# Moving the block exchange of an MLP's hidden layer from GpSimd's queue to SyncE's, with other buffers and take times

## The chip, the core and the metric

The kernel runs on one core of a Trainium2 chip. Its time is the device time of one execution in microseconds (us). Before the change it is 2130.66 us, the median of three runs (2129.62 to 2133.73). The engines are PE (TensorE), DVE (VectorE), ACT (ScalarE), POOL (GpSimd) and SP (SyncE). SP computes nothing here; it issues DMAs.

## The reference

Two transformer blocks follow each other on 256 tokens of width 2048, everything in fp32. Both end in an MLP with a squared ReLU and a hidden width of 8192; the change touches only these two MLPs.

```python
def sqrelu_mlp(h, w1, w2):                       # block 1
    return jnp.square(jax.nn.relu(h @ w1)) @ w2

x = x + g1 * rms_norm(fourier_mix(modulate(rms_norm(x, g), sh1, sc1)) @ fnet_w_out, g)
x = x + g2 * rms_norm(sqrelu_mlp(modulate(rms_norm(x, g), sh2, sc2), w_mlp_in, w_mlp_out), g)
# sh, sc, g1 and g2 are silu(c) @ w_mod + b_mod

x = x + mixed @ w_out                            # block 2: attention
u = jax.nn.relu(rmsnorm(x, g_mlp) @ w_up)
x = x + (u * u) @ w_down
return rmsnorm(x, g_final)
```

## The kernel before

**Weights.** Every weight is read once from HBM by SP in chunks of 1 MB: 512 rows by 512 columns, in a ring of four slots, `raw` (L334 to L343). Before it loads a slot again, SP waits until DVE has finished with the chunk four places earlier (`raw_used`). A chunk is used in two halves. For each half ACT rounds it to fp32r (`w_high`, `high_part`, L900), DVE subtracts for the rest (`w_low`, `low_part`, L1267), and PE multiplies three times (high by high, low by high, high by low; L495 to L497), which gives 12 matmuls of 512 columns. `w_high` and `w_low` have four slots (LEAD = 4), so ACT can prepare half n + 4 only once PE is done with half n.

**An MLP** is cut into four quarters of 2048 hidden columns. A quarter has 64 halves: 32 for the up projection, in four steps c = 0 to 3 of 512 columns (8 halves each), and 32 for the down projection. The order of the halves is a table (`QUARTER_ORDER`). The very first quarter has another (`FIRST_ORDER`): halves 0 to 11 are the first four of each of the steps 0, 1 and 2, halves 12 to 23 the last four of each, 24 to 31 step 3. So its steps end at halves 15, 19, 23 and 31, and those of the other quarters at 7, 15, 23 and 31. Loads of another weight (`w_mod`, for the vector g2) lie among the loads of the first two quarters: SP issues such a tile behind chunk pos + 2 for each pos in `MOD_FIRST` or `MOD_AFTER`, and DVE sums it up in one operation of 2048 columns (L1279).

**Turning the hidden layer.** The down projection needs the hidden values turned, so that hidden columns lie on the partitions. After the last half of a step, ACT applies ReLU (L982, L1019) and squares in place (`hidden`, L984, L1021), DVE transposes 32x32 blocks (`turn_blocks`, L1433) from `hidden` into `blocks`, and 16 DMAs of 32 KB (`exchange`, L436) bring the blocks from each group of 32 partitions to the others (`extra<-scr` in the profile: `exchanged` lies in `extra`, `hidden` and `blocks` in `scr`). Each moves one run of 256 numbers (1 KB) per partition. POOL issues them and does nothing else in that time. Then ACT copies the result into `u_high` (`take_exchanged`, L959) and DVE puts the rest into `u_low` (`take_low`, L1425). The tables `FIRST_TAKES` and `TAKES` say behind which half's weights ACT and DVE do this: 5, 6, 7 and 6 halves behind the end of steps 0 to 3 in the first quarter, and 6 halves behind it in all others. `FIRST_BLOCKS` puts the transposes 0, 1, 2 and 0 halves behind the end.

ACT and DVE execute what is written in their order. An ACT that waits for an exchange prepares no weights, and after four halves PE has none.

Of the kernel before, what the change touches and what calls it, by code (L numbers as in the profile page):

```python
# [29 lines left out]
TT = SEQ // P  # L30
KT = D // P
CW = 512
# [66 lines left out]
FIRST_TAKES = {y + d: c for c, (y, d) in enumerate(zip(FIRST_UP_ENDS, (5, 6, 7, 6)))}  # L99
FIRST_BLOCKS = {y + d: c for c, (y, d) in enumerate(zip(FIRST_UP_ENDS, (0, 1, 2, 0)))}  # L100
TAKES = {y + 6: c for c, y in enumerate(UP_ENDS)}
DOWN_ENDS = [QUARTER_ORDER.index((NC + c, HALVES - 1)) for c in range(NC)]
AFTER = {DOWN_ENDS[1] + 2: 0, DOWN_ENDS[1] + 4: 1, DOWN_ENDS[2] + 2: 2}
EARLY_UP = sum(unit == UP for unit, _ in FRONT)
# [5 lines left out]
RUN = TT * CW // QUADS  # L110
# [62 lines left out]
def program(nc, x, c_in, w_mod, b_mod, norm_g, w_mlp_in, w_mlp_out, fnet_w, g_attn, w_in, b_f,  # L173
# [8 lines left out]
    with ctx:  # L182
# [78 lines left out]
        hidden = scr[:, 0:TT * CW].rearrange("p (t n) -> p t n", t=TT)  # L261
        tables = extra[:, :].rearrange("p (t n) -> p t n", t=2)
        turned = extra[:, 0:2 * CW].rearrange("p (b n) -> p b n", b=2)
        blocks = scr[:, TT * CW:2 * TT * CW]
# [64 lines left out]
        def _(eng):  # L329
# [36 lines left out]

            for n, (unit, k) in enumerate(FRONT):
# [9 lines left out]
            for pos in range(EARLY_UP - 2, 32):  # L377
# [4 lines left out]
                if pos in MOD_FIRST:  # L382
                    mod_tile(G2, MOD_FIRST.index(pos))
            for pos in range(32):
# [4 lines left out]
                if pos in MOD_AFTER:  # L389
                    mod_tile(G2, len(MOD_FIRST) + MOD_AFTER.index(pos))  # L390
            for q in range(2, QUARTERS):
                for ch in range(2, 32):
                    mlp_chunk(w_mlp_in, w_mlp_out, q, ch)
                for j in range(2):
# [14 lines left out]
            with t.loop(eng, 0, QUARTERS - 1, raw=32) as q:  # L409
                for ch in range(2, 32):  # L410
                    mlp_chunk(w_up, w_down, q, ch)
                for j in range(2):
                    chunk(w_up, j * 4 * P, (q + 1) * D)
            for ch in range(2, 32):
                mlp_chunk(w_up, w_down, QUARTERS - 1, ch)

# [10 lines left out]
        def _(eng):  # L427
            t = Tally()

            def exchange(c):  # L430

                t.add("blocks")
                eng.wait_ge(t_blocks, t.c["blocks"])
                for a in range(QUADS):
                    for q in range(QUADS):
                        eng.dma_start(exchanged[q * BLOCK:(q + 1) * BLOCK, a * RUN:(a + 1) * RUN],  # L436
                                      blocks[a * BLOCK:(a + 1) * BLOCK, q * RUN:(q + 1) * RUN])\
                           .then_inc(t_exchanged[c % 2], 16)

# [21 lines left out]
            for q in range(QUARTERS):  # L461
                for c in range(NC):
                    exchange(c)
# [1339 lines left out]
```

## Time and profile before

| | us |
|---|---|
| median of three runs | 2130.66 |
| the profiled execution | 2133.73 |
| its span (first to last instruction) | 2131.9 |
| PE busy | 2040.6 |
| DVE busy | 1285.1 |
| ACT busy | 1029.4 |
| POOL busy (only issues and clears) | 273.1 |

The profiled execution is the slowest of the three runs. Its span and the 1.8 us around it make its time. PE's share of the span is 96%. Its mean granted clock is 0.984 of full speed. The stretch from about 311 to 402 us belongs to the first quarter of the first MLP, that up to 985 us to the rest of that MLP, 1000 to 1400 us to attention, and 1430 to 2115 us to the second MLP.

### The profile page before, as it was taken

To read this page: it belongs to the slowest core of one execution; us is meant where nothing else is said; L and a number is where in the kernel's file an instruction comes from. 1 tells how busy PE (TensorE), PEld (TensorE's weight loads), DVE (VectorE), ACT (ScalarE), POOL (GpSimd) and SP (SyncE) were. 2 spreads that over 40 slices of the span, in tenths; PEclk is the share of its full clock that TensorE was granted. 3 is DMA by queue.
4 is the path that set the end of the run, shared out by engine and by line. 5 is a ranking of instruction groups with operands and counts; after the bars stand their busy time and mean duration, and the time that the engine had idled before them with its cause. 6 is when DMAs were issued, how large, how long until landed. Compare 5 with 4: busy or idle time off the path is not lost.

```text
span 2131.9 us, 23074 instructions
## 1 busy us (share of the span) xinstructions
PE 2040.6 (96%) x8965; PEld 1652.8 (78%) x8965; DVE 1285.1 (60%) x1259; ACT 1029.4 (48%) x1350; POOL 273.1 (13%) x537
## 2 busy tenths in 40 slices
PE   3999879999999999998999999999999999999997
PEld 1776567788888888887788777788888888888886
DVE  7989776657665554556446555655555554554554
ACT  3333434445444544545555745555445544544553
POOL 0000014102202301210000000002202301310410
PEclk9899889999999999999999999999999999999999
DMA  9999897778766656664545444457656656666762
GB/s 401 408 384 365 318 342 254 269 244 271 268 233 194 221 198 203 212 198 137 178 158 170 146 158 158 159 177 217 217 190 203 219 197 203 214 200 193 225 207 99
DMA packets 214262, 480.23 MB, mean 225 GB/s; under 512 B 15592, under 2 KB 16040, under 8 KB 205328
## 3 DMA queue, kind: packets, MB, share of 16 engines
q1 hardware_dynamic: 195904, 455.11, 63.2%
q0 software_dynamic: 17232, 20.51, 3.3%
q10 hardware_dynamic: 1024, 3.20, 0.4%
q8 instruction: 71, 1.16, 0.2%
q14 instruction: 31, 0.25, 0.0%
HBM read 459.87 MB, written 2.10 MB: 217 GB/s over the span
## 4 chain that ended last, share of the span: by engine, by line
PE 80%; DVE 7%; DMA 7%; ACT 3%; issue 2%; POOL 1%; ACTq 0%; SPq 0%; DVEq 0%
PE ps L495 25%; PE ps L497 25%; PE ps L496 25%; DVE w_low L1267 2%; DVE scr L1279 2%; DMA raw<-in_fnet_w 2%; DMA raw<-in_w_mod 2%; DMA raw<-in_w_mlp_in 1%; POOL extra L436 1%; DVE scr L1294 1%; ACT w_high L900 1%; DMA extra<-scr 1%; PE ps L513 1%; PE ps L550 1%; PE ps L526 1%
## 5 line engine op out<-in xcount | busy, mean ns | idle before, releaser
L1267 DVE TENSOR_TENSOR w_low<-raw,w_high 128x1024 fp32r<-128x1024 f32 x672 | 817.0, 1222 | 676.1 <-ACT w_high L900 675.7
L900 ACT ACTIVATE w_high<-raw 128x1024 fp32r<-128x1024 f32 x672 | 706.2, 1058 | 881.0 <-PE ps L497 773.7
L495 PE MATMUL ps<-w_high,h_both 128*128 128x512 f32 x1536 | 608.9, 396 | 16.2 <-DVE w_low L1267 10.5
L497 PE MATMUL ps<-w_high,h_both 128*128 128x512 f32 x1536 | 600.9, 391 | 0.0
L496 PE MATMUL ps<-w_low,h_both 128*128 128x512 f32 x1536 | 600.7, 391 | 0.0
L495 PE MATMUL ps<-w_high,u_high 128*128 128x512 f32 x1152 | 449.7, 390 | 3.9 <-DVE w_low L1267 3.6
L497 PE MATMUL ps<-w_high,u_low 128*128 128x512 f32 x1152 | 448.3, 389 | 0.0
L496 PE MATMUL ps<-w_low,u_high 128*128 128x512 f32 x1152 | 448.3, 389 | 0.0
L436 POOL DMA_DIRECT2D extra<-scr x512 | 250.1, 497 | 1044.5 <-DVE scr L1433 800.2
L495 PEld LDWEIGHTS ps<-w_high,h_both 128*128 128x128 f32 x1536 | 290.4, 189 | 79.5 <-DVE w_low L1267 10.5
L497 PEld LDWEIGHTS ps<-w_high,h_both 128*128 128x128 f32 x1536 | 290.0, 189 | 61.5
L496 PEld LDWEIGHTS ps<-w_low,h_both 128*128 128x128 f32 x1536 | 290.6, 189 | 60.2 <-issue 1.4
L495 PEld LDWEIGHTS ps<-w_high,u_high 128*128 128x128 f32 x1152 | 216.3, 188 | 50.2 <-DVE w_low L1267 3.8
L497 PEld LDWEIGHTS ps<-w_high,u_low 128*128 128x128 f32 x1152 | 216.2, 188 | 45.0
L496 PEld LDWEIGHTS ps<-w_low,u_high 128*128 128x128 f32 x1152 | 216.3, 188 | 44.7
L1279 DVE SCALAR_TENSOR_TENSOR scr<-raw,silu_c,scr 128x2048 f32<-128x2048 f32 x64 | 150.4, 2351 | 10.6 <-DMA raw<-in_w_mod 5.5
L1294 DVE SCALAR_TENSOR_TENSOR scr<-raw,silu_c,scr 128x1024 f32<-128x1024 f32 x46 | 59.1, 1284 | 9.3 <-DMA raw<-in_w_mod 7.1
L1425 DVE TENSOR_TENSOR u_low<-extra,u_high 128x512 fp32r<-128x512 f32 x64 | 41.2, 686 | 30.3 <-ACT u_high L959 30.3
L1433 DVE STREAM_TRANSPOSE scr<-scr 128x512 f32<-128x512 f32 x64 | 41.8, 691 | 25.6 <-ACT scr L1021 24.0
L959 ACT ACTIVATE u_high<-extra 128x512 fp32r<-128x512 f32 x64 | 36.6, 619 | 39.6 <-DMA extra<-scr 39.6
L608 PE MATMUL ps<-extra,acc 128*128 128x512 f32 x64 | 31.3, 649 | 23.1 <-ACT acc L1050 23.1
L910 ACT ACTIVATE junk<-xs 128x512 f32<-128x512 f32 x64 | 40.4, 632 | 24.0 <-DVE xs L1405 16.0
(183 smaller groups left out, 846.2 us busy)
## 6 DMA issues: line engine op xcount, KB each, us to landing
raw<-in_w_mod SPq DMA_DIRECT2D x96, 1024.0 KB, 7.2
raw<-in_w_mlp_in SPq DMA_DIRECT2D x64, 1024.0 KB, 5.9
raw<-in_w_mlp_out SPq DMA_DIRECT2D x64, 1024.0 KB, 5.3
raw<-in_w_up SPq DMA_DIRECT2D x64, 1024.0 KB, 5.4
raw<-in_w_down SPq DMA_DIRECT2D x64, 1024.0 KB, 5.1
raw<-in_w_in SPq DMA_DIRECT2D x48, 1024.0 KB, 5.1
raw<-in_fnet_w SPq DMA_DIRECT2D x16, 1024.0 KB, 7.0
extra<-scr POOLq DMA_DIRECT2D x512, 32.0 KB, 3.9
```

What stands on the lines that cost most here:

```text
L436: eng.dma_start(exchanged[q * BLOCK:(q + 1) * BLOCK, a * RUN:(a + 1) * RUN], blocks[a * BLOCK:(a + 1) * BLOCK, q * RUN:(q + 1) * RUN])\
L495: eng.matmul(dst, ah, wh, start=(k == 0), stop=False)
L496: eng.matmul(dst, ah, wl, start=False, stop=False)
L497: last = eng.matmul(dst, al, wh, start=False, stop=(k == KT - 1))
L900: eng.activation(w_high[:, h % LEAD, :], raw[:, slot, (h % 2) * 2 * CW:(h % 2 + 1) * 2 * CW], ACT.Copy).then_inc(high_ready, 1)
L910: eng.activation(junk[:, :], src, ACT.Square, accum_out=ssq[:, column:column + 1])\
L959: eng.activation(dst, src[:, tt, :, :, :], ACT.Copy).then_inc(t_high, 1)
L1267: eng.tensor_tensor(w_low[:, h % LEAD, :], raw[:, slot, piece], w_high[:, h % LEAD, :].bitcast(f32), ALU.subtract).then_inc(raw_used if h ...
L1279: eng.scalar_tensor_tensor(out=mod_acc(v), in0=raw[:, slot, :], scalar=silu_c[:, bass.ds(kk, 1)], in1=mod_acc(v), op0=ALU.mult, op1=ALU.ad ...
L1294: ins = eng.scalar_tensor_tensor(out=sums, in0=raw[:, slot, k * HALF:(k + 1) * HALF], scalar=silu_c[:, 2 * r + k:2 * r + k + 1], in1=other ...
L1425: eng.tensor_tensor(low, src[:, tt, :, :, :], high.bitcast(f32), ALU.subtract).then_inc(t_low, 1)
L1433: last = eng.transpose(dst[:, tt, :, :, :], hidden[:, tt, :].rearrange("p (k q i) -> p k q i", k=4, q=QUADS))
```

## The change

- The 16 DMAs of an exchange are issued by SP. They stand in SP's order behind the load of chunk y // 2 + 6 of the quarter, where y is the half at which the step ends (`EXCHANGED_BEHIND = 6`), and behind a `w_mod` tile where one follows this chunk. The first waits for `t_blocks`, the semaphore of the block transposes.
- Each of them now moves four runs of 64 numbers (256 bytes) per partition on both sides, where it was one run of 256 numbers. `blocks` and `exchanged` are laid out accordingly: DVE's transposes write `128x16x32` in one pattern.
- `relu` and `hidden` are two buffers now; `blocks` shares its place with `relu`. ACT no longer waits for `t_blocks` ahead of the ReLU.
- The takes stand 4 halves behind the end of a step in the first quarter (before: 5, 6, 7, 6) and 5 in all others (before: 6). `FIRST_BLOCKS` is gone: the transposes stand at the end of the step itself.

```diff
-FIRST_TAKES = {y + d: c for c, (y, d) in enumerate(zip(FIRST_UP_ENDS, (5, 6, 7, 6)))}
-FIRST_BLOCKS = {y + d: c for c, (y, d) in enumerate(zip(FIRST_UP_ENDS, (0, 1, 2, 0)))}
-TAKES = {y + 6: c for c, y in enumerate(UP_ENDS)}
+FIRST_TAKES = {y + 4: c for c, y in enumerate(FIRST_UP_ENDS)}
+TAKES = {y + 5: c for c, y in enumerate(UP_ENDS)}
+EXCHANGED_BEHIND = 6
...
-        hidden = scr[:, 0:TT * CW].rearrange("p (t n) -> p t n", t=TT)
+        relu = scr[:, 0:TT * CW].rearrange("p (t n) -> p t n", t=TT)
+        hidden = scr[:, TT * CW:2 * TT * CW].rearrange("p (t n) -> p t n", t=TT)
-        blocks = scr[:, TT * CW:2 * TT * CW]
+        blocks = scr[:, 0:TT * CW]
...
+            def exchange(c):                       # on SP
+                t.add("blocks")
+                eng.wait_ge(t_blocks, t.at("blocks", 0))
+                for a in range(QUADS):
+                    src = blocks[a * BLOCK:(a + 1) * BLOCK, :].rearrange("p (k q n) -> p k q n", k=4, q=QUADS)
+                    for q in range(QUADS):
+                        dst = exchanged[q * BLOCK:(q + 1) * BLOCK, :].rearrange("p (k a n) -> p k a n", k=4, a=QUADS)
+                        eng.dma_start(dst[:, :, a, :], src[:, :, q, :]).then_inc(t_exchanged[c % 2], 16)
+            def exchange_behind(ch):
+                for c, y in enumerate(UP_ENDS):
+                    if ch == y // 2 + EXCHANGED_BEHIND:
+                        exchange(c)
...
                 if pos in MOD_FIRST:
                     mod_tile(G2, MOD_FIRST.index(pos))
+                for c, y in enumerate(FIRST_UP_ENDS):
+                    if pos + 2 == y // 2 + EXCHANGED_BEHIND:
+                        exchange(c)
...
                 if pos in MOD_AFTER:
                     mod_tile(G2, len(MOD_FIRST) + MOD_AFTER.index(pos))
+                exchange_behind(pos + 2)
...
-            def exchange(c):                       # on POOL
-                t.add("blocks")
-                eng.wait_ge(t_blocks, t.c["blocks"])
-                for a in range(QUADS):
-                    for q in range(QUADS):
-                        eng.dma_start(exchanged[q * BLOCK:(q + 1) * BLOCK, a * RUN:(a + 1) * RUN],
-                                      blocks[a * BLOCK:(a + 1) * BLOCK, q * RUN:(q + 1) * RUN])\
-                           .then_inc(t_exchanged[c % 2], 16)
...
-                            if t.c["up"] > 1:
-                                eng.wait_ge(t_blocks, t.c["up"] - 1)
-                            eng.activation(hidden, ps[:, bank:bank + 2, :], ACT.Relu).then_inc(up_taken, 1)
+                            eng.activation(relu, ps[:, bank:bank + 2, :], ACT.Relu).then_inc(up_taken, 1)
                             eng.wait_ge(up_taken, t.c["up"])
-                            eng.activation(hidden, hidden, ACT.Square).then_inc(up_ready, 1)
+                            eng.activation(hidden, relu, ACT.Square).then_inc(up_ready, 1)
...
-                dst = blocks.rearrange("p (q k t j) -> p t k q j", q=QUADS, k=4, t=TT)
+                dst = blocks.rearrange("p (b t j) -> p t b j", t=TT, j=BLOCK)
...
-                    if y in FIRST_BLOCKS:
+                    if hh == 7 and c < NC:
                         turn_blocks()
```

SP in the first quarter, from the `w_mod` tile behind chunk 10 on. `raw` is the ring of weight slots, `in_w_mlp_in` and `in_w_mlp_out` are the up and the down projection's weights. In the kernel before no exchange stands here:

```order
L342 DMA raw<-in_w_mod 128x2048 [waits raw_used]
L342 DMA raw<-in_w_mlp_in 128x4x512 [waits raw_used] x3
L342 DMA raw<-in_w_mod 128x2048 [waits raw_used]
L342 DMA raw<-in_w_mlp_in 128x4x512 [waits raw_used] x2
L342 DMA raw<-in_w_mlp_out 128x4x512 [waits raw_used]
L342 DMA raw<-in_w_mod 128x2048 [waits raw_used]
L342 DMA raw<-in_w_mlp_out 128x4x512 [waits raw_used] x3
```

The three loads in a row are chunks 11, 12 and 13; then come the tile behind chunk 13, chunks 14 and 15, chunk 16 with its tile, and chunks 17 to 19. In the changed kernel the same place reads:

```order
L342 DMA raw<-in_w_mod 128x2048 [waits raw_used]
L342 DMA raw<-in_w_mlp_in 128x4x512 [waits raw_used] x3
L342 DMA raw<-in_w_mod 128x2048 [waits raw_used]
L375 DMA extra<-scr 32x4x64 [waits t_blocks]
L375 DMA extra<-scr 32x4x64 x15
L342 DMA raw<-in_w_mlp_in 128x4x512 [waits raw_used] x2
L375 DMA extra<-scr 32x4x64 [waits t_blocks]
L375 DMA extra<-scr 32x4x64 x15
L342 DMA raw<-in_w_mlp_out 128x4x512 [waits raw_used]
L342 DMA raw<-in_w_mod 128x2048 [waits raw_used]
L342 DMA raw<-in_w_mlp_out 128x4x512 [waits raw_used]
L375 DMA extra<-scr 32x4x64 [waits t_blocks]
```

The exchanges of steps 0, 1 and 2 now stand behind a load that itself waits for DVE: the `w_mod` tile behind chunk 13, chunk 15 and chunk 17.

ACT in the first quarter, in the kernel before, from the ReLU of step 0 (`scr<-ps`) to the take of step 1 (`u_high<-extra`):

```order
L982 ACTIVATE scr<-ps 128x1024
L984 ACTIVATE scr<-scr 128x1024
L900 ACTIVATE w_high<-raw 128x1024 x4
L982 ACTIVATE scr<-ps 128x1024
L984 ACTIVATE scr<-scr 128x1024
L900 ACTIVATE w_high<-raw 128x1024
L959 ACTIVATE u_high<-extra 128x4x128 x2
L900 ACTIVATE w_high<-raw 128x1024 x3
L982 ACTIVATE scr<-ps 128x1024
L984 ACTIVATE scr<-scr 128x1024
L900 ACTIVATE w_high<-raw 128x1024 x2
L959 ACTIVATE u_high<-extra 128x4x128 x2
```

And in the changed kernel, from the same ReLU to the same take and the weights behind it:

```order
L984 ACTIVATE scr<-ps 128x1024
L986 ACTIVATE scr<-scr 128x1024
L904 ACTIVATE w_high<-raw 128x1024 x4
L963 ACTIVATE u_high<-extra 128x4x128 x2
L984 ACTIVATE scr<-ps 128x1024
L986 ACTIVATE scr<-scr 128x1024
L904 ACTIVATE w_high<-raw 128x1024 x4
L963 ACTIVATE u_high<-extra 128x4x128 x2
L984 ACTIVATE scr<-ps 128x1024
L986 ACTIVATE scr<-scr 128x1024
L904 ACTIVATE w_high<-raw 128x1024 x4
```

The take of step 0 was one weight half behind the ReLU and square of step 1 and is now ahead of them; the take of step 1 was two halves behind those of step 2 and is now ahead of them.

## Rows read from the trace of the kernel before

**Rows 1.** The page's part 1: busy time, share, instructions.
```profile
PE 2040.6 (96%) x8965; PEld 1652.8 (78%) x8965; DVE 1285.1 (60%) x1259; ACT 1029.4 (48%) x1350; POOL 273.1 (13%) x537
```

**Rows 2.** Busy time in stretches, then PE's granted clock, DMA share, GB/s.
```profile
402.00:985.00 583.00, 583.00 (x2566) 481.50 (x2566) 341.35 (x297) 282.45 (x322) 93.79 (x192) 1.00 0.70 226
1430.00:2115.00 685.00, 685.00 (x3024) 567.22 (x3023) 367.32 (x334) 336.82 (x391) 125.07 (x256) 1.00 0.63 200
```

**Rows 3.** PE from 343 to 385 us: start, time, idle before it.
```profile
365.05 0.50 PE L495 MATMUL ps<-w_high,h_both 128*128 128x512 f32 x1 [2.41 <-DVE w_low L1267]
382.35 0.50 PE L495 MATMUL ps<-w_high,u_high 128*128 128x512 f32 x1 [3.41 <-DVE w_low L1267]
```

**Rows 4.** All waits: us in total, times, longest.
```profile
ACT u_high L959 <- DMA extra<-scr: 39.6, 12, 9.7
```

**Rows 5.** ACT from 318 to 402 us, in order of time.
```profile
324.59 1.06 ACT L900 ACTIVATE w_high<-raw 128x1024 fp32r<-128x1024 f32 x1 [1.60 <-PE ps L497]
...
335.47 1.06 ACT L900 ACTIVATE w_high<-raw 128x1024 fp32r<-128x1024 f32 x1 [1.59 <-PE ps L497]
336.44 1.01 ACT L982 ACTIVATE scr<-ps 128x1024 f32<-128x1024 f32 x1
337.48 1.06 ACT L984 ACTIVATE scr<-scr 128x1024 f32<-128x1024 f32 x1
338.45 1.04 ACT L900 ACTIVATE w_high<-raw 128x1024 fp32r<-128x1024 f32 x1
342.64 1.15 ACT L959 ACTIVATE u_high<-extra 128x512 fp32r<-128x512 f32 x2 [3.15 <-DMA extra<-scr]
...
346.35 1.06 ACT L900 ACTIVATE w_high<-raw 128x1024 fp32r<-128x1024 f32 x1 [0.67 <-PE ps L497]
...
360.72 1.16 ACT L959 ACTIVATE u_high<-extra 128x512 fp32r<-128x512 f32 x2 [7.86 <-DMA extra<-scr]
...
378.95 1.15 ACT L959 ACTIVATE u_high<-extra 128x512 fp32r<-128x512 f32 x2 [9.72 <-DMA extra<-scr]
```

**Rows 6.** DVE from 318 to 402 us.
```profile
327.70 1.31 DVE L1433 STREAM_TRANSPOSE scr<-scr 128x512 f32<-128x512 f32 x2 [0.78 <-ACT scr L984]
...
332.49 2.35 DVE L1279 SCALAR_TENSOR_TENSOR scr<-raw,silu_c,scr 128x2048 f32<-128x2048 f32 x1
...
336.57 1.23 DVE L1267 TENSOR_TENSOR w_low<-raw,w_high 128x1024 fp32r<-128x1024 f32 x1 [0.59 <-ACT w_high L900]
...
343.30 1.30 DVE L1425 TENSOR_TENSOR u_low<-extra,u_high 128x512 fp32r<-128x512 f32 x2 [2.56 <-ACT u_high L959]
```

**Rows 7.** SP from 318 to 402 us; one row can hold several issues.
```profile
334.87 0.34 SPq L342 DMA_DIRECT2D raw<-in_w_mod  x1
337.82 9.49 SPq L342 DMA_DIRECT2D raw<-in_w_mlp_in  x2
```

**Rows 8.** Line 342: duration of an issue in ns, min/median/max.
```profile
L342 SPq DMA_DIRECT2D raw<-in_w_mod x96: 327/340/470, 0.8 to 595.4; - x96
L342 SPq DMA_DIRECT2D raw<-in_w_mlp_in x64: 367/368/467, 227.6 to 870.4; - x64
```

**Rows 9.** Line 436: the same, and the time from issue to landing.
```profile
L436 POOL DMA_DIRECT2D extra<-scr x512: 496/496/522, 329.3 to 2048.5; - x171
...
DMA to landing us min/median/max: 1.7/3.9/7.4
```

**Rows 10.** The chain of waits, 322 to 385 us: start, us, what.
```profile
336.64 5.97 DMA extra<-scr
...
353.42 7.28 DMA extra<-scr
```

**Rows 11.** DMA queues: packets, MB, share of 16 engines' span.
```profile
q0 software_dynamic: 17232, 20.51, 3.3%
```

**Rows 12.** PE from 990 to 1000 us, in order of time.
```profile
992.94 3.67 PE L550 MATMUL ps<-cst,xs 128*128 128x128 f32 x16 [5.21 <-DVE xs L1373]
```

**Rows 13.** Busy time in the ten us behind it; columns as in Rows 2.
```profile
992.00:1002.00 10.00, 8.10 (x27) 6.81 (x28) 9.44 (x17) 4.37 (x16) 0.00 (x0) 0.51 0.33 105
```

More of the change, by code:

```diff
@@ L109 @@
 QUADS = P // BLOCK
-RUN = TT * CW // QUADS
 MOVED = 16 * QUADS * QUADS * NC // 2
@@ L393, in _ @@
                     mlp_chunk(w_mlp_in, w_mlp_out, q, ch)
+                    exchange_behind(ch)
                 for j in range(2):
@@ L408, in _ @@
             chunk(w_up, 4 * P, 0)
-            with t.loop(eng, 0, QUARTERS - 1, raw=32) as q:
+            with t.loop(eng, 0, QUARTERS - 1, raw=32, blocks=NC) as q:
                 for ch in range(2, 32):
                     mlp_chunk(w_up, w_down, q, ch)
+                    exchange_behind(ch)
                 for j in range(2):
@@ L415, in _ @@
                 mlp_chunk(w_up, w_down, QUARTERS - 1, ch)
+                exchange_behind(ch)
             outv = out.rearrange("(t p) n -> p t n", p=P)
@@ L427, in _ @@
         def _(eng):
-            t = Tally()
-            def exchange(c):
-                t.add("blocks")
-                eng.wait_ge(t_blocks, t.c["blocks"])
-                for a in range(QUADS):
-                    for q in range(QUADS):
-                        eng.dma_start(exchanged[q * BLOCK:(q + 1) * BLOCK, a * RUN:(a + 1) * RUN],
-                                      blocks[a * BLOCK:(a + 1) * BLOCK, q * RUN:(q + 1) * RUN])\
-                           .then_inc(t_exchanged[c % 2], 16)
             for v, unit in enumerate(MOD_INIT):
@@ L460, in _ @@
             eng.memset(acc[:, :, :], 0.0).then_inc(acc_zero, 1)
-            for q in range(QUARTERS):
-                for c in range(NC):
-                    exchange(c)
             eng.wait_ge(mod_read, G2 + 1)
@@ L468, in _ @@
             eng.dma_start(grow[:, :], g_final.broadcast_to([P, D])).then_inc(grow_in, 16)
-            for q in range(QUARTERS):
-                for c in range(NC):
-                    exchange(c)
         @block.tensor
@@ L955, in take_exchanged @@
                 eng.wait_ge(t_exchanged[c % 2], 16 * QUADS * QUADS * (c // 2 + 1) + earlier)
-                src = exchanged.rearrange("p (a k t j) -> p t k a j", k=4, a=QUADS, t=TT)
+                src = exchanged.rearrange("p (k a t j) -> p t k a j", k=4, a=QUADS, t=TT)
                 for tt in range(TT):
@@ L1011, in mlp_body @@
                             t.add("up")
-                            eng.wait_ge(t_blocks, t.at("up", -1))
                             if scaled:
                                 for tt in range(TT):
-                                    last = eng.activation(hidden[:, tt, :], lin(c)[:, tt, :], ACT.Relu,
+                                    last = eng.activation(relu[:, tt, :], lin(c)[:, tt, :], ACT.Relu,
                                                           scale=rstd[:, tt:tt + 1])
@@ L1018, in mlp_body @@
                             else:
-                                eng.activation(hidden, lin(c), ACT.Relu).then_inc(up_taken, 1)
+                                eng.activation(relu, lin(c), ACT.Relu).then_inc(up_taken, 1)
                             eng.wait_ge(up_taken, t.at("up", 0))
-                            eng.activation(hidden, hidden, ACT.Square).then_inc(up_ready, 1)
+                            eng.activation(hidden, relu, ACT.Square).then_inc(up_ready, 1)
                         else:
@@ L1416, in take_low @@
             def take_low(c):
-                src = exchanged.rearrange("p (a k t j) -> p t k a j", k=4, a=QUADS, t=TT)
+                src = exchanged.rearrange("p (k a t j) -> p t k a j", k=4, a=QUADS, t=TT)
                 for tt in range(TT):
@@ L1430, in turn_blocks @@
                 eng.wait_ge(up_ready, t.at("up", 0))
-                dst = blocks.rearrange("p (q k t j) -> p t k q j", q=QUADS, k=4, t=TT)
+                dst = blocks.rearrange("p (b t j) -> p t b j", t=TT, j=BLOCK)
                 for tt in range(TT):
-                    last = eng.transpose(dst[:, tt, :, :, :],
-                                         hidden[:, tt, :].rearrange("p (k q i) -> p k q i", k=4, q=QUADS))
+                    last = eng.transpose(dst[:, tt, :, :], hidden[:, tt, :].rearrange("p (b i) -> p b i", i=BLOCK))
                 last.then_inc(t_blocks, 1)
```

## The prediction, made before the changed kernel was run

> **What bounds the kernel now.** I read the page's first part, then stretches of time, then what PE waited for. PE is busy for 96% of the span [rows 1], and in the two long stretches that hold 7 of the 8 MLP quarters it is never idle: 583.00 of 583.00 us and 685.00 of 685.00 us [rows 2]. POOL's exchanges, DVE's transposes and ACT's copies all lie in these stretches too, and cost nothing. The first of them gives the kernel's beat: 583.00 us over 2566 matmuls is 0.227 us each, so a half (12 matmuls) takes 2.73 us and a chunk 5.45 us. What the change can win must therefore lie in the first quarter, from 311 to 402 us. There PE waits twice for DVE's `w_low`, 2.41 and 3.41 us, and once more for 0.2 [rows 3]: 6.0 us together. DVE waits for ACT, and ACT for the exchange: 39.6 us over the whole kernel, of which 3.15, 7.86 and 9.72 us stand at the takes of steps 0, 1 and 2 [rows 4, 5]. POOL is slow at this, 16 issues of 0.496 us or 7.9 us [rows 9], and behind its last issue the data still took 5.97 and 7.28 us to land [rows 10]. The gain can be no more than 6.0 us, 0.28% of the time. The loss has no such bound.
>
> **The change, part by part.**
>
> *Quarters without these stalls (7 of 8).* Behind the end of a step ACT needs about 2.1 us for ReLU and square [rows 5] and DVE 1.3 for the transposes [rows 6], so the blocks are ready some 4.5 us behind the end. SP by then has loaded the chunk ahead and issues 16 DMAs. One issue costs SP 0.34 us for a tile in 128 long rows and 0.37 for a chunk in 512 short ones [rows 8]; the new DMAs have 128 pieces, so I take 0.37, or 5.9 us for 16. With some 2 us until the last has landed (POOL's shortest are 1.7 [rows 9], when nothing is queued) an exchange takes L = 7.9 us and ends 12.4 us behind the step. ACT comes to its take when the copy behind half 5 is made, 5 x 2.73 + 1.0 = 14.6 us behind it. Nobody waits. SP's next load can be late by about 3 us, but a load is needed three chunks (16 us) later: hidden. In the second quarter the `w_mod` tiles push the exchange back; the worst is step 1, where it stands behind a tile that waits until DVE is done with the tile three chunks earlier, 10.1 us behind the step. There it ends at 18.3, ACT waits 3.7 us, and PE's four prepared halves last until 24.5: hidden, as long as L stays under about 10.6. So these edits cost 0. The dropped wait for `t_blocks`, the second buffer, the other pattern of the transposes (the same 512 numbers per operation) also get 0: ACT and DVE are 48% and 60% busy, PE's work hides them. POOL's 250 us of issues go, but no engine waited for POOL other than by the exchange.
>
> *The first quarter.* Its steps end only 4 halves (10.9 us) apart, and here the exchange now starts late and the take stands early. I follow it with these durations: copy high 1.0, ReLU 1.0, square 1.05, take 1.15 on ACT; `take_low` and the transposes 1.3 each, `w_low` 1.2, a `w_mod` tile 2.35 on DVE [rows 5, 6].
>
> Step 0. Half 15 ends at 324.5 and half 19 at 335.4, when ACT starts the next copies [rows 5]. SP reaches the exchange behind the tile of chunk 13, which it can issue only when DVE is done with the tile before (332.49 + 2.35); it did so at 334.87 [rows 6, 7]. The exchange runs 335.2 to 341.1 and has landed by 343.0. POOL's landed at 342.6, so nothing is won. But ACT now meets this take ahead of the ReLU of step 1 and ahead of the copy for half 24, which before stood at 338.45. It waits from 336.4 to 343.0, does take, ReLU and square until 346.2 and the copy until 347.1; DVE's transposes end at 347.5 and `w_low` of half 24 at 348.7. PE was done with half 23 at 346.3 [rows 5]: it waits 2.4 us.
>
> Step 1. Its exchange stands behind chunk 15, which needs DVE's second half of chunk 12, done at 349.9. It runs from 350.6 to 356.5 and lands at 358.5. Then take, ReLU of step 2, square, copy (362.6), and on DVE `w_low` at 364.2. PE, started again at 348.7, runs out at 359.6: it waits 4.6 us.
>
> Step 2. Behind chunk 17, which needs half 29 on DVE, done at 365.4: exchange 366.0 to 371.9, landed 373.9. No ReLU stands behind this take; the weights of half 32 are ready at 377.2, PE is out at 375.1: 2.1 us. Step 3 (take at half 35, landed about 393.4, PE served until 399) costs nothing, and neither does its missing wait of 3.41.
>
> The sum: 2.4 + 4.6 + 2.1 = 9.1 us of idle PE instead of 6.0, so +3.1 us. It depends on L: each us of L comes three times, as each exchange starts only when the weights behind the last one are made.
>
> *Bounds for L.* The landing behind the last issue was 5.97 and 7.28 us in this place [rows 10]; but there three or four MB of loads had been issued beside it, while now SP cannot issue loads while it issues the exchange. From below: issues of 0.34 and a landing of 1.7 make L = 7.1. If the issue went by the number of pieces it would be 0.09 us and L = 3.2, but 128 rows take 0.34 and 512 pieces 0.37, so it hardly does [rows 8]. From above: POOL's 0.496 for an issue would make 9.9. The transfer itself: a packet of POOL's queue took 0.033 x 16 x 2131.9 / 17232 = 65 ns on an engine [rows 11]. Each engine now has 8 pieces of 256 bytes per DMA. If each is as dear as such a packet that is 0.52 us, more than the 0.37 of an issue, and 16 take 8.3 us: L = 10.3. If only the bytes count, the issue sets the pace and L stays. I keep 7.9, nearest to the issue rows, and 3.2 to 10.3 as ends.
>
> The Trainium skill says on "DMA: Bandwidth & Descriptors" (Specifications) that transfers reach full rate only from 512 bytes a piece, since below that the engine reads, modifies and writes. The 256-byte pieces fall under it; by that rule the case of L = 10.3 is the one to expect. No run of before has such pieces, so the trace neither confirms nor denies it.
> The skill's "SBUF — State Buffer" (SBUF: two separate sides) says that descriptors of a GpSimd DMA starve while DVE holds the shared port, and to issue from SP or ACT instead. Here POOL's 512 issues took 496 to 522 ns whatever DVE did [rows 9]; by the rule the move would win more than I give it, by the row it wins nothing of this kind.
>
> **Rivals.**
> - *PE's clock falls (slower).* The stall of 4.6 us lies between those of 2.41 and 3.41, over which the trace shows no drop, and one of 5.21 us [rows 3, 12], behind which PE ran 10 us at half clock, 1.2 instead of 2.4 GHz [rows 13]. That costs 5 us of work; it would eat the third stall of 2.1, so +2.9 on top: +6.0.
> - *Pieces or issues are dearer (slower).* L = 10.3 gives 3 x 2.4 = +7.2 more: +10.3. It decides from L = 8.3 on (+4.3). For it: 65 ns for a packet. Against it: that mean is over larger packets. If L passes 10.6, the second quarter adds a stall too.
> - *The exchange is quicker (faster).* An L of 3.2 ends all stalls: -6.0, the whole of what there is. It needs issues of less than 0.2 us, against the rows. L = 5.9 leaves 0.4 + 2.6 + 0.1 = 3.1 us of stalls: -2.9.
> - *The change does not do what it says:* SP, held by its wait for `t_blocks`, would delay the loads instead. Against it: wherever an exchange stands, the load ahead of it waits for DVE work that stands behind the same transposes or ends just ahead of them, so SP waits 1 to 2 us at most: +0 to it.
>
> **How the numbers follow.** Two runs of this kernel can be told apart from 0.2% on, about 4.3 us. The forecast (+3.1, between 0 and +4.3) gets 0.45, the clock 0.20, dearer pieces or issues 0.15, quicker or unmoved 0.20, of which half beyond -4.3 us. That is faster 0.10, same 0.55, slower 0.35. The profiled execution would go from 2133.73 to 2136.8; it was the slowest of three, 3.07 above their median of 2130.66. On the median the forecast is 2130.7 + 3.1 = 2133.8. The range: from 2127.5 (-3.2, L = 5.8, between forecast and the quicker case) to 2142 (+11, dearer pieces); 0.1 below and 0.1 above are left out.
>
> **What would show it right or wrong.** Right: SP issues of 0.37 us; the first exchange issued at about 335 and the second behind chunk 15; ACT waits of some 6.6, 8 and 8 us at the takes of steps 0 to 2; three PE idles near 346, 360 and 375 with a sum of 9; none from 402 to 985 and from 1430 to 2115. Wrong: an issue far from 0.37; landings of more than 3 us behind the last issue; a clock drop between 360 and 380; PE idle in the second quarter, or a beat other than 0.227 us, which nothing here foresees.

## The result, and the profile after

The changed kernel takes 2160.49 us (median of four runs, 2158.97 to 2162.16); the kernel before, run beside it, 2131.08 us (2129.62 to 2133.73). The ratio is 1.0137, with a 95% interval of 1.0119 to 1.0154: slower by some 29 us, far outside the range of 2127.5 to 2142.

The profiled execution of the changed kernel took 2156.88 us, with a span of 2155.1; it was its fastest, and that of before was its slowest. So the two traces show 23.2 us of the 29.4 between the medians, and the rest lies between runs of the same kernel (the changed one's other runs had a mean granted clock of 0.979 to 0.981, the profiled one 0.982).

The page's part 1 for the kernel after, which answers to [rows 1]:

```profile
PE 2047.8 (95%) x8965; PEld 1654.5 (77%) x8965; DVE 1286.5 (60%) x1259; ACT 1027.6 (48%) x1350; POOL 22.9 (1%) x25
```

PE does the same 8965 matmuls in 7.2 us more of busy time, and is idle for 107.3 us of the span instead of 91.3: 16.0 more. 7.2 + 16.0 = 23.2 is the whole difference. All waits of PE for `w_low` and of ACT for the exchange, after and then before (us in total, times, longest):

```profile
ACT u_high L963 <- DMA extra<-scr: 117.1, 32, 12.0
...
PE ps L499 <- DVE w_low L1268: 31.9, 15, 7.4
```
```profile
PE ps L495 <- DVE w_low L1267: 14.1, 8, 3.4
```

ACT now waits at every one of the 32 takes, three times as long in sum as in [rows 4], and PE waits 17.8 us more. Where PE waits, in order of time (start, duration, and in brackets the idle time before and its releaser):

```profile
351.62 0.76 PE L499 MATMUL ps<-w_high,h_both 128*128 128x512 f32 x1 [7.42 <-DVE w_low L1268]
370.42 0.80 PE L499 MATMUL ps<-w_high,h_both 128*128 128x512 f32 x1 [5.90 <-DVE w_low L1268]
387.07 0.76 PE L499 MATMUL ps<-w_high,u_high 128*128 128x512 f32 x1 [2.94 <-DVE w_low L1268]
413.37 0.50 PE L499 MATMUL ps<-w_high,u_high 128*128 128x512 f32 x1 [1.49 <-DVE w_low L1268]
...
549.62 0.52 PE L499 MATMUL ps<-w_high,h_both 128*128 128x512 f32 x1 [2.68 <-DVE w_low L1268]
```

The first four are the steps of the first quarter, 17.75 us where before it was 6.0 ([rows 3] and a third one of 0.2); the fifth is step 1 of the second quarter, which with four small ones behind it makes 5.3 us where before there was none. The reason is in SP's order of time (start, duration of the group, number of issues), which answers to [rows 7]:

```profile
332.74 0.34 SPq L342 DMA_DIRECT2D raw<-in_w_mod  x1
333.13 11.42 SPq L375 DMA_DIRECT2D extra<-scr  x16
344.59 8.41 SPq L342 DMA_DIRECT2D raw<-in_w_mlp_in  x2
353.05 10.38 SPq L375 DMA_DIRECT2D extra<-scr  x16
...
371.94 10.27 SPq L375 DMA_DIRECT2D extra<-scr  x16
```

The place is the one forecast: behind the `w_mod` tile, behind chunk 15, behind chunk 17. Sixteen issues take 10.3 to 11.4 us instead of the 5.9 forecast. By the line (duration of one issue in ns, min/median/max, then issue to landing), as in [rows 8, 9]:

```profile
L375 SPq DMA_DIRECT2D extra<-scr x512: 585/601/1619, 333.1 to 2071.3; - x171
...
DMA to landing us min/median/max: 1.9/1.9/6.5
```

The chain of waits shows how such issues follow each other (start, duration), in the second exchange:

```profile
353.69 0.60 SPq L375
354.33 0.60 SPq L375
354.98 0.60 SPq L375
355.62 0.60 SPq L375
...
362.83 1.92 DMA extra<-scr
```

They stand 0.645 us apart: 0.60 of issue and 0.045 between. The landing behind the last one is 1.92 us, as forecast. From the first issue (333.13, 353.05, 371.94) to ACT's take this gives L = 12.75, 11.7 and 11.6 us.

That is long against the forecast of 7.9, but not against the kernel before. There the exchange of step 0 went out from 329.30 on and was taken at 342.64 [rows 5], 13.3 us later, and those of steps 1 and 2 took 14.6 and 14.8 us: POOL's issues are shorter, but behind the last of them the landing took 5.97 and 7.28 us [rows 10] where it is 1.92 now. What got worse is the start. POOL began 0.3 us behind the end of the transposes (its exchange in the kernel before, then the transposes of step 1 in the changed one):

```profile
329.30 7.85 POOL L436 DMA_DIRECT2D extra<-scr  x16 [12.75 <-DVE scr L1433]
```
```profile
349.06 1.31 DVE L1434 STREAM_TRANSPOSE scr<-scr 128x512 f32<-128x512 f32 x2 [1.22 <-ACT scr L986]
```

These transposes end at 350.37, and SP begins at 353.05, 2.7 us later. At step 2 it is 2.7 us too, at step 0 it is 6.2. ACT, which answers to [rows 5]:

```profile
333.35 1.06 ACT L904 ACTIVATE w_high<-raw 128x1024 fp32r<-128x1024 f32 x1 [1.60 <-PE ps L501]
345.88 1.15 ACT L963 ACTIVATE u_high<-extra 128x512 fp32r<-128x512 f32 x2 [11.47 <-DMA extra<-scr]
346.93 1.00 ACT L984 ACTIVATE scr<-ps 128x1024 f32<-128x1024 f32 x1
347.97 1.06 ACT L986 ACTIVATE scr<-scr 128x1024 f32<-128x1024 f32 x1
348.93 3.88 ACT L904 ACTIVATE w_high<-raw 128x1024 fp32r<-128x1024 f32 x4
```

Between 334.4 and 345.9 ACT does nothing; ReLU, square and four halves of weights stand behind the take and are then made at one go. That is the mechanism forecast, with 11.47 us in the place of 6.6.

Last, the clock, in stretches (PE busy is the second number, PE's granted clock the third from the end), which answers to [rows 13]:

```profile
344.00:352.00 8.00, 0.58 (x2) 0.42 (x2) 4.24 (x6) 6.09 (x8) 0.00 (x0) 0.79 0.49 142
352.00:356.00 4.00, 4.00 (x12) 3.10 (x12) 3.90 (x4) 0.81 (x1) 0.00 (x0) 0.57 0.56 124
...
371.00:376.00 5.00, 5.00 (x13) 3.91 (x12) 2.77 (x3) 0.71 (x1) 0.00 (x0) 0.51 0.65 213
...
387.00:392.00 5.00, 4.93 (x12) 3.89 (x13) 4.90 (x4) 3.48 (x4) 0.00 (x0) 0.50 0.55 172
```

Behind each of the first three idles PE runs some 4 to 6 us at 1.2 instead of 2.4 GHz: 12 matmuls in 4 us, then 13 and 12 in 5 us, where full clock holds 18 and 22. With a shorter stretch behind the idle of 549.62 this costs some 8.6 us by the count of matmuls; elsewhere the trace has 1.4 us less than that of before, which leaves the 7.2 us of busy time. The first matmul behind the idle tells it too: 0.76 to 0.80 us there, 0.50 behind the idle of 1.49.

### The profile page after: what moved, and what is told of

It reads as the page before. It is cut to its first block, busy times and chain, and to the rows that moved or that the text cites. A ratio compares the mean times of both kernels' runs of the same rounds, so it can differ in the third digit from the quotient of the medians.

```text
span 2155.1 us, 23055 instructions
## 1 busy us (share of the span) xinstructions
PE 2047.8 (95%) x8965; PEld 1654.5 (77%) x8965; DVE 1286.5 (60%) x1259; ACT 1027.6 (48%) x1350; POOL 22.9 (1%) x25
## 4 chain that ended last, share of the span: by engine, by line
PE 75%; DVE 9%; DMA 6%; SPq 4%; ACT 3%; issue 2%; ACTq 0%; DVEq 0%
PE ps L499 24%; PE ps L500 24%; PE ps L501 24%; DVE w_low L1268 4%; SPq L375 4%; DVE scr L1280 3%; DMA raw<-in_w_mod 2%; DMA raw<-in_fnet_w 2%; DMA raw<-in_w_mlp_in 1%; ACT w_high L904 1%; DVE scr L1295 1%; PE ps L517 1%; PE ps L554 1%; DMA extra<-scr 1%; DVE scr L1434 0%
## 5 line engine op out<-in xcount | busy, mean ns | idle before, releaser
L612 PEld LDWEIGHTS ps<-extra,acc 128*128 128x128 f32 x64 | 13.9, 221 | 40.2 <-issue 40.2
```

What stands on the lines that cost most here:

```text
L612: last = eng.matmul(side(2 * (g % 2) + d), acc[:, tt, k * P:(k + 1) * P], tables[:, tt, 0:2 * SEQ], start=(tt == 0), stop=(tt == 1))
```

## The experiments

Theory 1, after the result: SP's issue of this kind of DMA costs about 0.6 us by itself, and the late place and the early takes turn the longer exchange into stalls. Rivals: the 256-byte pieces make it dear (2); the takes' new place alone makes the stalls (3).

**The pieces.** The changed kernel with one run of 1 KB per partition again.

```diff
-eng.dma_start(dst[:, :, a, :], src[:, :, q, :]).then_inc(t_exchanged[c % 2], 16)
+eng.dma_start(exchanged[q * BLOCK:(q + 1) * BLOCK, a * RUN:(a + 1) * RUN],
+              blocks[a * BLOCK:(a + 1) * BLOCK, q * RUN:(q + 1) * RUN]).then_inc(t_exchanged[c % 2], 16)
```

> The changed kernel, but each of SP's 16 DMAs of an exchange moves one run of 1 KB per partition again, as POOL's did (the layouts and the transposes' pattern are those of before). Place in SP's order, buffers and takes stay changed. Theory 1, SP cannot issue DMAs back to back faster than one in 0.60 to 0.65 us whatever they hold: issues stay at 0.60 us, time 2156 to 2163. Theory 2, the four short runs per partition make an issue dear: issues fall to about 0.37 us, an exchange lands 8 us after its first issue, and the time falls to 2132 to 2140.

It took 2154.27 us, 1.0103 [1.0078, 1.0127] of before, just below the range of theory 1. Its issues:

```profile
L374 SPq DMA_DIRECT2D extra<-scr x512: 508/591/1759, 334.1 to 2069.6; - x171
```

0.591 instead of 0.601 us, and PE idles of 7.26, 4.72, 3.55 and 1.37 us in the first quarter. The pieces are not the cause of the dear issue. Since the changed kernel had run on another chip, both were later run on one:

> The changed kernel once more, on one chip with the next one, to size the pieces. All theories: a ratio of 1.010 to 1.014 to the kernel before.

> The changed kernel with runs of 1 KB instead of four pieces of 256 bytes, once more, beside the changed kernel on the same chip. Theory 1, pieces cost 10 ns per issue and nothing else: 0 to 1.5 us less than the changed kernel. Theory 2, pieces cost the DMA engines time that the chain pays: 4 us or more less.

2159.56 us (1.0128 [1.0111, 1.0145]) with pieces of 256 bytes, 2158.31 us (1.0113 [1.0096, 1.0130]) with 1 KB. The intervals overlap: what the pieces cost is not told from nothing. The other side of the same question is the kernel before, POOL issuing, with pieces of 256 bytes and nothing else changed:

> The kernel before with POOL issuing, but in the changed layout: four runs of 256 bytes per partition. Theory 1, short pieces cost the DMA engines little (19 ns each in the changed kernel): POOL's issue grows by less than 0.1 us from 0.50, time 2129 to 2135. Theory 2, pieces cost at the descriptor generation: an issue of 0.7 us or more, an exchange of 13 us or more to its landing, time 2140 or more.

2136.66 us, 1.0014 [1.0004, 1.0023]. POOL's issue went from 0.496 to 0.549 us:

```profile
L438 POOL DMA_DIRECT2D extra<-scr x512: 549/549/572, 330.5 to 2051.5; - x171
```

So pieces cost POOL 0.053 us an issue, 0.8 us an exchange, and SP 0.010. With POOL they show in the time: from first issue to take the exchanges of steps 0 to 2 lasted 14.4, 15.6 and 16.6 us (before 13.3, 14.6 and 14.8), PE's two idles are 4.54 and 3.73 us (before 2.41 and 3.41), and the whole is some 3 us longer, with an interval that leaves out 1.

**The order of the work.** Two kernels part the engine from the order. In the first SP issues, in pieces and in the changed place, but buffers, waits, transposes and takes are those of before.

```diff
-FIRST_TAKES = {y + 4: c for c, y in enumerate(FIRST_UP_ENDS)}
-TAKES = {y + 5: c for c, y in enumerate(UP_ENDS)}
+FIRST_TAKES = {y + d: c for c, (y, d) in enumerate(zip(FIRST_UP_ENDS, (5, 6, 7, 6)))}
+FIRST_BLOCKS = {y + d: c for c, (y, d) in enumerate(zip(FIRST_UP_ENDS, (0, 1, 2, 0)))}
+TAKES = {y + 6: c for c, y in enumerate(UP_ENDS)}
```

> SP issues the exchanges in 256-byte pieces at the changed place, but buffers, wait for t_blocks, takes (5, 6, 7, 6 and 6 halves behind the step) and FIRST_BLOCKS are those of before. Theory 1, the slow exchange hurts mostly because the take now stands ahead of the next ReLU and of the weights: PE idles 6 to 8 us in the first quarter, none or under 1 us in the second, time 2131 to 2137. Theory 2, the slow exchange alone explains the loss, wherever the take stands: time 2150 or more.

2135.98 us, 1.0013 [1.0003, 1.0023]. The issue is as dear as ever, the exchanges as long (11.47, 10.30, 10.30, 10.42 us), and most of the loss is gone:

```profile
L375 SPq DMA_DIRECT2D extra<-scr x512: 585/601/1672, 333.6 to 2047.6; - x171
```
```profile
350.73 0.50 PE L499 MATMUL ps<-w_high,h_both 128*128 128x512 f32 x1 [3.34 <-DVE w_low L1271]
...
367.11 0.50 PE L499 MATMUL ps<-w_high,h_both 128*128 128x512 f32 x1 [2.48 <-DVE w_low L1271]
381.88 0.50 PE L499 MATMUL ps<-w_high,u_high 128*128 128x512 f32 x1 [0.88 <-DVE w_low L1271]
385.15 0.47 PE L499 MATMUL ps<-w_high,u_high 128*128 128x512 f32 x1 [0.24 <-DVE w_low L1271]
```

In the second POOL issues runs of 1 KB as before, but the buffers and takes are the changed ones.

> The kernel before, POOL issuing 1 KB runs, but with the changed buffers, takes (4 and 5 halves behind the step) and the transposes at the step's end. Theory 1, the early takes cost by themselves: by the chain, stalls of about 2, 6.6 and 4.7 us in the first quarter (13 in place of 6) and 3 us of clock, time 2138 to 2143. Theory 2, only the issuing engine matters: time 2129 to 2134.

2145.62 us, 1.0052 [1.0035, 1.0069], above the 2138 to 2143 written ahead; the PE idles are 2.58, 5.54, 2.23 and 2.99 us, and ACT again waits at all 32 takes (105.8 us). The early takes cost some 11 us even without SP; with SP's exchange 29; SP's exchange with the old order 3. Theories 1 and 3 each hold half: together the two cost twice their sum. What SP adds is not a longer exchange, since POOL's here took 13.8, 13.6 and 12.3 us from first issue to take. It is the late start: from the end of the transposes to the take it is 14.1, 13.9 and 12.6 us here, and 19.0, 14.4 and 14.3 in the changed kernel.

**The place.** The changed kernel with the exchange one chunk (two halves) earlier in SP's order.

```diff
-EXCHANGED_BEHIND = 6
+EXCHANGED_BEHIND = 5
```

> The changed kernel with each exchange one chunk earlier in SP's order (EXCHANGED_BEHIND = 5), so that SP reaches it before the transposes are done and starts as soon as they are. Theory 1, the late start behind a load that waits for DVE is a large part of the loss: each first-quarter exchange starts about 4 us earlier, PE's idles of 7.4, 5.9, 2.9 and 1.5 us fall to about 3.4, 2, 0 and 0, the second quarter's 5.3 vanish, no clock drop: 2134 to 2142. Theory 2, SP now blocks the loads behind it, which costs as much: 2150 or more.

2134.70 us, 1.0002 [0.9992, 1.0012]: the whole loss is gone, though each exchange still takes 10.3 us. SP now begins as soon as the transposes end, and from there to the take it is 11.7, 11.6 and 11.6 us. So in this place SP's exchange serves the early takes better than POOL's did; it is the late start that made a loss of it. ACT waits (4.22, 8.35, 9.15, 7.17), and of PE's idles one large one is left:

```profile
362.20 0.79 PE L499 MATMUL ps<-w_high,h_both 128*128 128x512 f32 x1 [4.86 <-DVE w_low L1268]
376.14 0.47 PE L499 MATMUL ps<-w_high,u_high 128*128 128x512 f32 x1 [1.27 <-DVE w_low L1268]
...
398.96 0.50 PE L499 MATMUL ps<-w_high,u_high 128*128 128x512 f32 x1 [0.81 <-DVE w_low L1268]
```

The second quarter has none: PE is busy 218.00 of 218.00 us from 402 to 620, where the changed kernel has 211.22. The reverse test leaves the place and puts only the takes of the later quarters (`TAKES`) back from 5 to 6 halves:

> The changed kernel, but in all quarters other than the first the takes stand 6 halves behind the step again (changed: 5). Theory 1, the second quarter's idles (5.3 us, with a short clock drop) come from this half: 4 to 6 us less than the changed kernel, 2154 to 2157, first quarter unchanged. Theory 2, they come from the slow exchange only: within 2 us of the changed kernel.

2153.84 us, 1.0100 [1.0083, 1.0117]. The second quarter's idle falls from 5.3 to 1.0 us, and the clock no longer drops there; the first quarter keeps its own (7.60, 5.42, 4.01, 1.51). So that is a term of some 4 us of idle, 6 to 8 us of time by the ratios (against 1.0128 and 1.0137 of the changed kernel), and the first quarter holds the rest.

**The length L.** The changed kernel with 8 of the 16 DMAs, so that an exchange takes about what I had forecast.

```diff
-                for a in range(QUADS):
+                for a in range(2):
```

> The changed kernel with only 8 of the 16 DMAs of each exchange, so half of the turned hidden values are not moved and the output is another. It halves the suspected cost alone. If PE's idles go by three times the length of an exchange (12.7 to 7 us), those of the first quarter fall from 17.7 to about 2.5 us and the second quarter's to 0, and the clock stays up: 2126 to 2131. If the early takes cost by themselves, whatever the length: 2140 or more.

2133.20 us, 1.0004 [0.9995, 1.0014]. From first issue to take: 335.80 to 343.74 = 7.9 us, then 7.6 and 6.8. PE's idles:

```profile
349.49 0.77 PE L499 MATMUL ps<-w_high,h_both 128*128 128x512 f32 x1 [2.63 <-DVE w_low L1268]
364.14 0.50 PE L499 MATMUL ps<-w_high,h_both 128*128 128x512 f32 x1 [1.95 <-DVE w_low L1268]
...
376.01 0.47 PE L499 MATMUL ps<-w_high,u_high 128*128 128x512 f32 x1 [0.69 <-DVE w_low L1268]
```

Forecast for L = 7.9 were 2.4, 4.6 and 2.1. The first is met. The others are smaller since L was, and since PE ran some 3 us at half clock behind the first (its 0.77 us tell it; the mean from 325 to 430 is 0.98), which makes four prepared halves last longer. The second quarter has no idle. Both guesses written ahead missed: the idles are 5.3 us and not 2.5, and the time lies between the two ranges. Yet with about the L that I had assumed the loss is gone: 0.9 us more than before by the ratio, where the prediction had 3.1.

**Why 0.6.** Three runs on the issue itself. In the first, SP waits in the first MLP for the landing of each of the first three DMAs of an exchange, so that the second, third and fourth go out alone.

> The changed kernel, but in the first MLP SP waits for the landing of the first, second and third DMA of each exchange before it issues the next, so that the second, third and fourth are issued alone. Theory 1, back-to-back issue is what costs: these three take about 0.37 us, the others 0.60. Theory 2, the shape costs (32 partitions, several dimensions): they take 0.60 too. The time, some 6 us longer per exchange, is of no interest.

One run, 2263.85 us. An exchange now lasts longer by the waits:

```profile
336.44 18.38 SPq L375 DMA_DIRECT2D extra<-scr  x16
```
```profile
L375 SPq DMA_DIRECT2D extra<-scr x512: 585/601/1541, 336.4 to 2178.3; - x171
```

The lone issues took 0.585 to 0.592 us, those in a burst 0.601. So for DMAs of this shape the price is not one of a queue that fills up. The second run moves 128 partitions of 256 bytes each instead of 32 of four times 256, inside SBUF still (nothing changes partitions):

```diff
+piece = slice((a * QUADS + q) * 64, (a * QUADS + q + 1) * 64)
+eng.dma_start(exchanged[:, piece], blocks[:, piece]).then_inc(t_exchanged[c % 2], 16)
```

> The changed kernel, but each of SP's 16 DMAs moves 64 numbers (256 bytes) of all 128 partitions from blocks to exchanged, in place of four such pieces of 32 partitions: the same 32 KB and the same 128 pieces, SBUF to SBUF, but no block changes its partitions, so the output is another. Theory 1, an issue is dear because the DMA touches 32 partitions only (or has more dimensions): 0.34 to 0.37 us, an exchange of 7.5 to 8 us, and with it a time of 2131 to 2135. Theory 2, SBUF as the source is what costs: 0.6 us and 2154 to 2160.

2157.83 us, 1.0108 [1.0090, 1.0126]; the exchanges took 11.27, 10.18 and 10.17 us, and the issue's median is 0.601 again:

```profile
L374 SPq DMA_DIRECT2D extra<-scr x512: 465/601/1993, 335.5 to 2072.4; - x171
```

But its minimum is 0.465. The first issue of an exchange, where SP has issued nothing for 1.7 us or more, takes 0.47 us here, 0.51 with runs of 1 KB and 0.60 in the changed kernel. So the shape does count for a lone issue, and no longer in a burst. The third keeps the shape and takes other data, from `w_mod` in HBM:

```diff
-src = blocks[a * BLOCK:(a + 1) * BLOCK, :].rearrange("p (k q n) -> p k q n", k=4, q=QUADS)
+src = w_mod[q * BLOCK:(q + 1) * BLOCK, 0:TT * CW].rearrange("p (k a n) -> p k a n", k=4, a=QUADS)
```

> The changed kernel, but the 16 DMAs of an exchange read their numbers from w_mod in HBM, in the same shape (32 partitions, four pieces of 256 bytes), so the hidden values are others and the output too. Theory 1, shape sets the issue: 0.6 us. Theory 2, an SBUF source does: 0.37 us, and the exchange is as short as a landing from HBM allows.

2144.41 us, 1.0040 [1.0026, 1.0053]:

```profile
L375 SPq DMA_DIRECT2D extra<-in_w_mod x512: 311/432/1803, 337.2 to 2057.9; - x171
...
DMA to landing us min/median/max: 1.7/2.1/5.6
```

The median falls to 0.432 us, an exchange to 7.7 to 8.9 us, and PE's idles to 4.99, 2.77, 3.04 and 1.52. A lone first issue takes 0.33 to 0.34 us. So most of what an issue costs above the 0.37 of [rows 8] goes with the source: out of SBUF 0.60, out of HBM 0.33 alone and 0.43 in a burst. Why, no run here shows, and two rows forbid a simple rule. The four stores at the end of the program, out of SBUF into HBM, begin with an issue of 0.36 us, so a source in SBUF is not dear by itself. And a load out of HBM pays too when SP issues it directly behind an exchange. The loads behind the second exchange of the changed kernel, then the same load behind an exchange out of HBM:

```profile
363.48 0.59 SPq L342 DMA_DIRECT2D raw<-in_w_mlp_out  x1
364.11 0.50 SPq L342 DMA_DIRECT2D raw<-in_w_mod  x1
```
```profile
362.56 0.43 SPq L342 DMA_DIRECT2D raw<-in_w_mlp_out  x1
```

Alone such a load costs 0.37 and a `w_mod` tile 0.34. All 19 loads directly behind an exchange of the changed kernel took 0.59 us. In a row, then, an issue costs what goes with the DMA ahead of it: 0.58 to 0.60 us behind one from SBUF to SBUF in all these kernels, 0.43 behind one of 32 KB out of HBM.

**A better version.** If SP's issue is 0.60 and POOL's 0.50 and both can issue at once, half the DMAs each should take 8 x 0.645 = 5.2 us. Into the kernel before (its buffers, takes and runs of 1 KB) SP is put with the DMAs of the last two groups of 32 partitions, behind chunk y // 2 + 5, with semaphores of its own; POOL keeps the first two.

```diff
+EXCHANGED_BEHIND = 5
...
-                for a in range(QUADS):             # on POOL
+                for a in range(2):
...
+                for a in range(2, QUADS):          # on SP, behind chunk y // 2 + 5
...
-                eng.wait_ge(t_exchanged[c % 2], 16 * QUADS * QUADS * (c // 2 + 1) + earlier)
+                for moved in (t_exchanged, t_exchanged_sp):
+                    eng.wait_ge(moved[c % 2], 16 * 8 * (c // 2 + 1) + earlier)
```

> Buffers, takes and layout (1 KB runs) of before, but POOL issues 8 of the 16 DMAs of an exchange and SP the other 8, behind chunk y // 2 + 5. If the issue is what makes an exchange long, 8 issues take 4.0 us on POOL and 5.2 on SP, an exchange lands 6.5 us after its start, ACT waits under 2 us at each take, and PE's two idles of before (6.0 us) vanish: 2124 to 2129, a ratio of 0.997. If the DMA engines or the landing set it, an exchange still takes 10 us or more: 2131 to 2135.

2126.69 us, 0.9968 [0.9958, 0.9979]: faster than both kernels. Both queues issue side by side, and from 325 to 430 us PE is never idle:

```profile
326.33 5.04 SPq L375 DMA_DIRECT2D extra<-scr  x8
```
```profile
326.59 3.95 POOL L460 DMA_DIRECT2D extra<-scr  x8 [13.40 <-DVE scr L1458]
```
```profile
325.00:430.00 105.00, 105.00 (x465) 86.98 (x464) 74.05 (x64) 53.68 (x61) 15.69 (x32) 1.00 0.80 273
```

The take of step 0 begins at 336.69 and those of the next three steps at 350.06, 365.82 and 382.70, none of them with a wait for the exchange. The gain, 6.3 us against its own runs of before, is about the 6.0 that the prediction named as the most there is.

The last kernel leaves all 16 on SP, 1 KB runs, behind chunk y // 2 + 5, with the order of before.

> Buffers, takes and layout (1 KB runs) of before; SP issues all 16 DMAs, behind chunk y // 2 + 5, and POOL none. It tells whether the gain of the split kernel came from the split or from place and order. Theory 1, an exchange that starts with the transposes and lands 11.7 us later is in time for the old takes: ACT waits 1 to 4 us per take, PE idles under 1 us in the first quarter, 2125 to 2129, a ratio of 0.997. Theory 2, only a short exchange of 6.5 us gains: 2131 to 2136.

2129.32 us, 0.9980 [0.9970, 0.9989], whose interval meets that of the split. ACT's waits for the exchange fall to 4.2 us in all ([rows 4] has 39.6), and one idle of PE is left in the first quarter:

```profile
377.59 0.47 PE L500 MATMUL ps<-w_high,u_high 128*128 128x512 f32 x1 [2.76 <-DVE w_low L1272]
```

So the move to SP as such is a small gain, if it stands where the blocks get ready and the takes stay late. What the split adds to that is told by the idle (none in place of 2.76 us, behind which the clock dropped too) more than by the time.

| kernel | us | ratio to before | PE's idles in the first quarter |
|---|---|---|---|
| the change | 2160.49 | 1.0137 | 7.4, 5.9, 2.9, 1.5 |
| 1 KB runs | 2154.27 | 1.0103 | 7.3, 4.7, 3.6, 1.4 |
| SP, order of before | 2135.98 | 1.0013 | 3.3, 2.5, 0.9, 0.2 |
| POOL, changed order | 2145.62 | 1.0052 | 2.6, 5.5, 2.2, 3.0 |
| POOL, order of before, 256-byte pieces | 2136.66 | 1.0014 | 4.5, 3.7 |
| one chunk earlier | 2134.70 | 1.0002 | 0.2, 4.9, 1.3, 0.8 |
| later takes in the other quarters | 2153.84 | 1.0100 | 7.6, 5.4, 4.0, 1.5 |
| half of the DMAs | 2133.20 | 1.0004 | 2.6, 2.0, 0.7 |
| all 128 partitions | 2157.83 | 1.0108 | 7.3, 5.8, 2.8, 2.5 |
| source in HBM | 2144.41 | 1.0040 | 5.0, 2.8, 3.0, 1.5 |
| SP, earlier, order of before | 2129.32 | 0.9980 | 2.8 |
| half SP, half POOL | 2126.69 | 0.9968 | none |

## Why the prediction was wrong, step by step

- *What bounds the kernel.* Right: everything is decided by the first quarter, and 6.0 us is the most to be won; the split version wins it.
- *Seven quarters at no cost.* Right for six of them: PE is busy 345.00 of 345.00 us from 640 to 985 and 665.00 of 665.00 from 1450 to 2115. The second quarter failed, in the way named: "hidden, as long as L stays under about 10.6". L was about 12, and the idles are 5.3 us.
- *The places.* Right: the exchange of step 0 went out at 333.13, 0.4 us behind its tile, and the others behind chunks 15 and 17.
- *The step that failed:* "One issue costs SP 0.34 us for a tile in 128 long rows and 0.37 for a chunk in 512 short ones; the new DMAs have 128 pieces, so I take 0.37, or 5.9 us for 16." Issues took 0.60 us with 0.045 between, 10.3 us for 16; one of 1.62 in the first exchange made it 11.4. Both rows were medians of loads out of HBM, nearly all issued one at a time. I scaled them by the number of pieces, which [rows 8] show to matter little, and not by what differed: the source, and 16 issues in a row. The run out of HBM with the same shape (0.33 alone, 0.43 in a row) against that out of SBUF (0.60) shows both. The low price had to pay for the late start: the forecast let the exchange of step 0 land at 343.0, level with POOL's at 342.6, and with 0.6 us an issue it could not. No row of before gave the price. Its only SP issues out of SBUF, the four stores at the end of the program, took 0.36, 0.43, 0.78 and 1.19 us one after the other:

```profile
L422 SPq DMA_DIRECT2D out_x<-acc x4: 360/607/1190, 2125.0 to 2126.7; - x4
```

- *The bounds for L* (3.2 to 10.3) failed with it. The upper end took POOL's 0.496 as the dearest issue; another engine's price bounds nothing. The 0.045 us between two issues, 0.7 us an exchange, were in neither end. The landing (1.92 us, forecast 2) was right.
- *The three stalls.* For L = 12.75 my own rule gives 2.4 + 4.85 = 7.25 us at step 0; the trace has 7.42. At steps 1 and 2 it gives 8.4 and 5.8; the trace has 5.90 and 2.94, and of the 2.5 and 2.9 missing most is what PE lost at half clock just ahead of them (12 matmuls from 351.6 to 356 and 13 from 370.4 to 376, where full clock holds 19 and 25: 1.7 and 2.6 us). "Each us of L comes three times" held for idle and slow clock taken together. Step 3, forecast free, cost 1.49.
- *The rivals.* "PE's clock falls" came true, four times over, at 7.2 us in all. "Pieces or issues are dearer" had the right sign and consequence, but the pieces were not it. The rule of the Trainium skill's "DMA: Bandwidth & Descriptors" (Specifications) on pieces under 512 bytes, by which L = 10.3 was the case to expect, isn't borne out as a price that counts on SP: 256 bytes and 1 KB differ by 0.010 us an issue and by 1.3 us in the whole time, within the intervals. On POOL the pieces cost some 3 us; whether by that rule or by the longer issue, no run shows. Nor does any run show POOL's issues held up by DVE, as the Trainium skill's "SBUF — State Buffer" (SBUF: two separate sides) would have it: the split kernel's are 496 to 522 ns long.
- *The chances.* The dearer issue and the slower clock had 0.15 and 0.20, taken as cases apart. They are one: a longer L makes longer idles, and longer idles lower the clock. An unknown that enters three times and then once more through the clock needed a range at least up to where the second quarter joins in.

What stays open: why an issue from SBUF to SBUF, and the one directly behind it, is dearer on SP; whether it takes both ends in SBUF, as the stores suggest; what the single issues of 1.5 to 2.0 us inside a burst are (in the line views of all these kernels as the maximum, with both sources); and the 6 us by which the two medians differ more than the two profiled executions.

## What to carry to other kernels

Price a DMA that moves to another queue by an issue of the same kind on that queue (same memory at both ends, and with another issue directly ahead if it will stand in a row), count the time between issues too, and where no such row exists let the upper end be open, not another engine's price. An exchange that one engine waits for in its order costs by its length times the number of steps that follow close upon each other, so place its issue where its data get ready (here worth some 26 us by one constant), and the take behind the work that others need. Many small copies can be split over two issuing engines.

## What the runs showed of the hardware

- A lone SP issue cost 0.34 to 0.37 us for loads of 1 MB out of HBM and 0.33 for 32 KB out of HBM. For 32 KB from SBUF to SBUF it cost 0.47 us over 128 partitions, 0.51 as 32 runs of 1 KB and 0.585 to 0.60 in 128 pieces on 32 partitions.
- Directly behind another issue SP's cost went with the DMA ahead: 0.43 us behind 32 KB out of HBM, 0.58 to 0.60 behind 32 KB from SBUF to SBUF, whatever the shape, and even for a load out of HBM. POOL's issues cost 0.496, and 0.549 in four pieces per partition, in bursts.
- Behind the last issue an exchange landed 1.92 us later when SP, which issues the loads too, had issued it, and 5.97 and 7.28 us later when POOL had and SP went on loading beside it.
- The length of an idle alone did not tell what PE's clock did behind it: it fell behind 7.42, 5.90, 2.94 and 2.68 us after the change, behind 2.63 with half of the DMAs and, some 1.5 us later, behind 2.76 with SP earlier and the order of before; it did not behind 2.41 and 3.41 before, nor behind 3.34 with SP and the order of before, nor behind 3.04 with the source in HBM.
